# The fifth product of each quad as one 512-column product, with VectorE adding its halves, in a two-layer decoder trunk

## Chip, cores and metric

One Trainium2 chip, one core. The metric is the device time of one execution of the whole kernel in microseconds (us).

## The reference

The kernel computes a two-layer decoder trunk on 512 tokens of width 1024, batch 1, in float32. Each layer is a token mixer (layer 0: a gated linear recurrence beside dilated attention; layer 1: sliding-window attention with sinks), then cross-attention into 256 memory tokens, then a SwiGLU feed-forward block, each behind an RMSNorm and with a residual add. A last RMSNorm follows. What the change touches is the first half of the feed-forward block:

```python
def swiglu(h, w_gate_up, w_down):
    gate, up = jnp.split(h @ w_gate_up, 2, axis=-1)
    return (jax.nn.silu(gate) * up) @ w_down
```

with `h` 512 x 1024, `w_gate_up` 1024 x 5632 and `w_down` 2816 x 1024.

## The kernel before, in words

**Three products for one.** Each float32 matrix is split into a high part (rounded to the matmul's float32r) and a low part (the rest), and a product is the sum high x high + high x low + low x high. The activations are kept with tokens in the free dimension.

**Quads.** The feed-forward block of a layer works on its 22 tiles of 128 hidden columns in two chunks, of 12 and 10 tiles. The first three pairs of tiles of the first chunk are done plainly (`plain_gate`, `plain_up`, `plain_product`, `plain_low` on VectorE, `plain_silu`, `plain_high` on ScalarE). All others are done as *quads*: a quad is a product of 256 output columns (two tiles, of the gate in an even quad, of the up projection in the following odd one) by a Strassen-like scheme of seven block products instead of eight. A chunk's quads form a *run*: 6 quads in the first run of each layer, 10 in the second, 32 in all. A run is followed by the down projection of its chunk (lines 815, 818 and 819 on TensorE).

Each of the seven kinds of product multiplies sums of weight blocks (4 blocks of 128 x 128) with sums of activation blocks (4 of 128 x 256). The kinds in `APART` have the low and the high activations side by side, so that one matmul of 512 columns (line 992) gives high weights x low activations in the left half of a PSUM bank and high x high in the right half. Four matmuls of 256 columns with the low weights (line 984) follow, onto the left half. The fifth kind is not among them before: it has two matmuls of 256 columns onto the same half bank (lines 1001 and 1002), and then line 984.

**Who makes the operands.** Per quad, VectorE makes four sums of weight blocks (`weight_sum`, line 2143) and seven low parts (`weight_low`, line 2148); ScalarE makes seven high parts (`weight_high`, line 2735). VectorE then forms the two output tiles from PSUM: `first_tile` (line 2177), `second_tile` (2185) and `second_tile_apart` (2191); it multiplies gate and up (`gated`, line 2199) and takes the low part of the result (`f_low`, line 2206), twice per two quads each. ScalarE does the SiLU (line 2786), the high part of the result (line 2780) and the copies: `copy_first` (fills the left half of bank 2 with zeros, line 2744, and copies bank 1 into bank 0, line 2746), `copy_fifth` (the fifth product into `copied`, line 2762), `copy_second_sum` (the second sum's left half into `copied`, line 2767, and its right half into the right half of bank 2, line 2768), `copy_third_sum` (line 2773) and `copy_apart` (line 2754).

**The order.** It is written out by hand, one list for each engine. TensorE in a run: product 1 of quad 0, then per quad 5, 6, 2, 3, 7, product 1 of the next quad, and 4 (in the last quad 5, 6, 2, 7, 3, 4). It waits for the high and low weights of each product (`HIGH`, `LOW`), before 5 for the zeros, before 6 for the copy of the first product, before 3 (in the last quad before 7) for the second copy of the second sum, before 4 for the third sum's. VectorE's list is the loop in `quads` from line 2209: in iteration n it makes low parts 6, 3, 7 and 4 of quad n and the sums and low parts 1, 5 and 2 of quad n + 1, with the tile work between. An odd iteration has 14 instructions, an even one 18 (from the third quad on). In iteration 0 of the first run of a layer, VectorE calls `rest()`, the six instructions of the last plain pair, of which the last two, the products, wait for two SiLU; ScalarE issues these two in its own `rest()`, behind `copy_fifth`. ScalarE's list is the loop from line 2789.

The weights of a quad come in two DMAs of 512 KB (line 606), issued on SyncE when the quad before last has done with the buffer. GpSimd makes the high parts of the other weights (line 737) and does nothing within a run but its end.

Of the kernel before, what the change touches and what calls it, by code (L numbers as in the profile page):

```python
# [69 lines left out]
Z_HIGHS = (1, 2, 4, 5, 6, 7, 3)  # L70
APART = (1, 2, 3, 4, 6, 7)
Z_STEP = {slot: 2 if slot in [Z_SLOT[i] for i in APART] else 1 for slot in range(8)}
# [92 lines left out]
LOW = counts((1, 5, 2, 6, 3, 7), ((0, 6), (1, 1), (0, 3), (0, 7), (0, 4), (1, 5), (1, 2)))  # L165
COPIED = counts(("zero", "c1"), ((0, "c5"), (0, "u2"), (0, "u2d"), (0, "u3"), (1, "zero"), (1, "c1")))

# [28 lines left out]
def trunk(nc, x, mem, w_in, w_gates, w_out0, w_qkv, w_out1, xa_wq, xa_wkv, xa_wo, w_gate_up, w_down,  # L196
          vectors, gains, mask0, mask1, rope_cos, rope_sin, identity, out):
    ctx = ExitStack()
    with ctx:
# [80 lines left out]
        quad_v_lo = at("quad_v_lo", [P, 2, 4, 4, P], F32R, z_x)  # L280
        copied = at("copied", [P, 2, QHALF], F32, z_mv)
        apart = at("apart", [P, 2, QHALF], F32, z_mv + 2048)

# [524 lines left out]
        def _(pe):  # L808
# [186 lines left out]

            def quad_product(l, q, i, o):

                quad_high_ready(l, q, i)
                lo, hi = z_rows(i)
                for k in range(4):  # L1000
                    pe.matmul(o, kind_hi(i)[:, k, :], zq_r[:, hi, :][:, k, :], start=False, stop=False, skip_group_check=True)  # L1001
                    pe.matmul(o, kind_hi(i)[:, k, :], zq_r[:, lo, :][:, k, :], start=False, stop=False, skip_group_check=True)  # L1002
                quad_low_weights(q, i, o)

            def quads(l, c):

                g0, n_quads = GROUP0[f"quads{l}{c}"], QUADS[c]

                def first_product(n):

                    pe.wait_ge(s_free[(g0 + n) % 2], free_needed(g0 + n))
                    quad_product_apart(l, QUAD0[l, c] + n, 1, ps[:, bank(g0 + n, 1), :], home(g0, n, 1), True)

                first_product(0)
                for n in range(n_quads):
                    q = QUAD0[l, c] + n
                    b, a, d = home(g0, n, 0), home(g0, n, 1), home(g0, n, 2)
                    b_wide, a_wide, d_wide = (ps[:, bank(g0 + n, i), :] for i in (0, 1, 2))
                    pe.wait_ge(s_cp, COPIED[q, "zero"])
                    quad_product(l, q, 5, d)  # L1020
                    pe.wait_ge(s_cp, COPIED[q, "c1"])
                    quad_product_apart(l, q, 6, a_wide, a)
                    quad_product_apart(l, q, 2, b_wide, b)
                    if n + 1 < n_quads:
                        pe.wait_ge(s_cp, COPIED[q, "u2d"])
                        quad_product_apart(l, q, 3, d_wide, d)
                        quad_product_apart(l, q, 7, a_wide, a)
                        first_product(n + 1)
                    else:
                        pe.wait_ge(s_cp, COPIED[q, "u2d"])  # L1030
# [467 lines left out]
        def _(dve):  # L1498
# [427 lines left out]
            for l in (0, 1):  # L1926
# [236 lines left out]
                def quads(c, rest, later):  # L2163
# [4 lines left out]
                    def free(n):  # L2168

                        dve.wait_ge(s_c, 3 * (QUAD0[l, c] + n) + 3)  # L2170
                        dve.nop().then_inc(s_free[(qg + n) % 2], 4)

                    def first_tile(n):
# [3 lines left out]
                        dve.tensor_tensor(halves(ff[:, 0, :]), bank_pair(qg, n, 0), apart[:], ALU.add).then_inc(s_c, 1)  # L2177

                    def second_tile(n):

                        q = QUAD0[l, c] + n
                        ff = ff_u if n % 2 else ff_g
                        dve.wait_ge(s_p, DONE[q, 3])
                        dve.wait_ge(s_cp, COPIED[q, "u3"])
                        dve.tensor_tensor(halves(ff[:, 1, :]), bank_pair(qg, n, 2), copied[:], ALU.add).then_inc(s_c, 1)

                    def second_tile_apart(n):

                        ff = ff_u if n % 2 else ff_g
                        dve.wait_ge(s_c, 3 * (QUAD0[l, c] + n) + 1)  # L2190
                        dve.tensor_tensor(halves(ff[:, 1, :]), halves(ff[:, 1, :]), bank_pair(qg, n, 2, 1),
                                          ALU.add).then_inc(s_c, 1)

                    def gated(n, p):

                        q = QUAD0[l, c] + n
                        dve.wait_ge(s_c, 3 * q + 3 - p)
                        dve.wait_ge(s_q_silu, 2 * (q // 2) + 2 - p)
                        dve.tensor_tensor(ff_u[:, p, :], ff_g[:, p, :], ff_u[:, p, :], ALU.mult).then_inc(s_q_prod, 1)
# [9 lines left out]
                    for n in range(n_quads):  # L2209
# [33 lines left out]
                        else:  # L2243
                            low_to(down0 + 2)
                        if more:
                            weight_low(q + 1, 5)
                            if n and not up:
                                f_low(n - 1, 0)
# [76 lines left out]
        def _(act):  # L2325
# [254 lines left out]
            for l in (0, 1):  # L2580
# [156 lines left out]
                def quads(c, rest, later):  # L2737
# [3 lines left out]
                    def copy_first(n):  # L2741

                        act.wait_ge(s_free[(qg + n) % 2], free_needed(qg + n))
                        act.activation(home(qg, n, 2), cos_t[:, 0:QHALF], ACT.Copy, scale=0.0).then_inc(s_cp, 1)
                        act.wait_ge(s_p, DONE[QUAD0[l, c] + n, 1])
                        act.activation(ps[:, bank(qg + n, 0), :], ps[:, bank(qg + n, 1), :], ACT.Copy).then_inc(s_cp, 1)

                    def copy_apart(n):
# [3 lines left out]
                        if q:  # L2752
                            act.wait_ge(s_c, 3 * q)
                        act.activation(apart[:], bank_pair(qg, n, 0, 1), ACT.Copy).then_inc(s_apart, 1)

                    def copy_fifth(n):
# [3 lines left out]
                        if q:  # L2760
                            act.wait_ge(s_c, 3 * q - 2)
                        act.activation(copied[:, 1, :], home(qg, n, 2), ACT.Copy).then_inc(s_cp, 1)

                    def copy_second_sum(n):

                        act.wait_ge(s_p, DONE[QUAD0[l, c] + n, 6])
                        act.activation(copied[:, 0, :], home(qg, n, 1), ACT.Copy).then_inc(s_cp, 1)
                        act.activation(home(qg, n, 2, 1), home(qg, n, 1, 1), ACT.Copy).then_inc(s_cp, 1)

# [12 lines left out]
                    def silu(n, p):  # L2782

                        q = QUAD0[l, c] + n
                        act.wait_ge(s_c, 3 * q if p == 0 else 3 * q + 2)
                        act.activation(ff_g[:, p, :], ff_g[:, p, :], ACT.Silu).then_inc(s_q_silu, 1)

                    copy_first(0)
                    for n in range(n_quads):
# [145 lines left out]
```

## Time and profile before

| what | us |
|---|---|
| median of 3 runs | 1286.35 (1286.25 to 1286.98) |
| the profiled execution | 1286.37 |
| its span in the trace | 1284.6 |
| TensorE busy in the span | 1277.1 (99%) |
| VectorE busy | 931.2 (72%) |
| ScalarE busy | 585.5 (46%) |
| GpSimd busy | 255.6 (20%) |

Busy times count a matmul from its start to its modelled end, and instructions overlap: the time from one start to the next is shorter than the duration of one. In a timeline row the first number is the start and the second the duration, in us; a row of several instructions covers them all. L992 is line 992 of the kernel; PE is TensorE, PEld its weight load, DVE VectorE, ACT ScalarE.

### The profile page before, as it was taken

What the parts mean: (1) busy time and instruction counts of PE and PEld (TensorE: products, weight loads), DVE (VectorE), ACT (ScalarE), POOL (GpSimd) and SP (SyncE); (2) the same over time, 40 slices, a digit from 0 to 9 for tenths busy, and PEclk for the clock granted to TensorE, in tenths of its full rate; (3) what the DMA queues carried; (4) which work ended last, traced back from release to release, by engine and by line L of the source; (5) the groups of instructions that cost most, each with busy time, mean ns of one, the idle gap of its engine ahead of it and who ended that gap; (6) DMA issues with size and microseconds to landing.
All of it is one profiled execution on the core that took longest, in us unless ns stands there. A gap on an engine that the chain in (4) does not pass through costs nothing.

```text
span 1284.6 us, 18398 instructions
## 1 busy us (share of the span) xinstructions
PE 1277.1 (99%) x6780; PEld 1073.4 (84%) x6780; DVE 931.2 (72%) x1445; ACT 585.5 (46%) x1194; POOL 255.6 (20%) x290
## 2 busy tenths in 40 slices
PE   9999999999999999999999999999999999999998
PEld 7888778888888888888888878888888888888886
DVE  7887856447689994389955778557789993489942
ACT  6347356114533671067722347425433760178712
POOL 0222254312422002100021226413321002000020
PEclk9999999999999999999999999999999999999999
DMA  7334323232333333333323332132333332343222
GB/s 250 97 100 115 91 67 99 81 92 91 116 98 99 118 96 99 98 115 99 104 93 115 107 117 60 50 98 88 110 97 94 116 93 96 97 132 99 83 98 98
DMA packets 96839, 130.63 MB, mean 102 GB/s; under 512 B 5328, under 2 KB 62160, under 8 KB 96752
## 3 DMA queue, kind: packets, MB, share of 16 engines
q1 hardware_dynamic: 94976, 127.29, 31.6%
q10 hardware_dynamic: 1776, 2.18, 0.6%
q8 instruction: 54, 0.88, 0.3%
q14 instruction: 33, 0.27, 0.1%
HBM read 124.67 MB, written 2.10 MB: 99 GB/s over the span
## 4 chain that ended last, share of the span: by engine, by line
PE 98%; DVE 1%; DMA 0%; ACT 0%; SPq 0%; issue 0%; ACTq 0%; POOL 0%; DVEq 0%; POOLq 0%
PE ps L815 18%; PE ps L819 18%; PE ps L818 18%; PE ps L992 14%; PE ps L984 8%; PE ps L1480 1%; PE ps L1476 1%; PE ps L1479 1%; PE ps L1309 1%; PE ps L1002 1%; PE ps L1001 1%; PE ps L1325 1%; PE ps L1338 1%; PE ps L1198 1%; PE ps L1229 1%; PE ps L1216 1%
## 5 line engine op out<-in xcount | busy, mean ns | idle before, releaser
L737 POOL TENSOR_SCALAR w_hi<-raw 128x1024 fp32r<-128x1024 f32 x156 | 182.3, 1169 | 928.0 <-PE ps L984 360.8
L1508 DVE TENSOR_TENSOR w_lo<-raw,w_hi 128x1024 fp32r<-128x1024 f32 x161 | 198.7, 1238 | 179.9 <-POOL w_hi L737 176.7
L815 PE MATMUL ps<-f_hi,w_hi 128*128 128x512 f32 x720 | 281.1, 390 | 0.2 <-DVEq L1904 0.2
L819 PE MATMUL ps<-f_hi,w_lo 128*128 128x512 f32 x720 | 280.3, 389 | 0.0
L818 PE MATMUL ps<-f_lo,w_hi 128*128 128x512 f32 x720 | 280.2, 389 | 0.0
L992 PE MATMUL ps<-zq_r,quad_hi 128*128 128x512 f32 x768 | 209.6, 394 | 0.0
L815 PEld LDWEIGHTS ps<-f_hi,w_hi 128*128 128x128 f32 x720 | 135.2, 188 | 28.8 <-DVEq L1904 0.4
L819 PEld LDWEIGHTS ps<-f_hi,w_lo 128*128 128x128 f32 x720 | 135.1, 188 | 28.3
L818 PEld LDWEIGHTS ps<-f_lo,w_hi 128*128 128x128 f32 x720 | 135.2, 188 | 27.7
L992 PEld LDWEIGHTS ps<-zq_r,quad_hi 128*128 128x128 f32 x768 | 131.5, 189 | 17.9
L815 PE MATMUL ps<-z_hi,w_hi 128*128 128x512 f32 x304 | 120.4, 396 | 0.0
L819 PE MATMUL ps<-z_hi,w_lo 128*128 128x512 f32 x304 | 118.4, 390 | 0.0
L818 PE MATMUL ps<-z_lo,w_hi 128*128 128x512 f32 x304 | 118.3, 389 | 0.0
L2735 ACT ACTIVATE quad_hi<-quad_raw 128x512 fp32r<-128x512 f32 x96 | 60.3, 628 | 114.6 <-DMA quad_raw<-in_w_gate_up 108.4
L2148 DVE TENSOR_TENSOR quad_v_lo<-quad_v,quad_hi 128x512 fp32r<-128x512 f32 x128 | 86.1, 693 | 0.0
L984 PEld LDWEIGHTS ps<-zq_r,quad_v_lo 128*128 128x128 f32 x512 | 76.6, 190 | 8.2
L2735 ACT ACTIVATE quad_hi<-quad_v 128x512 fp32r<-128x512 f32 x128 | 76.6, 621 | 13.6 <-DVE quad_v L2143 13.5
L984 PE MATMUL ps<-zq_r,quad_v_lo 128*128 128x256 f32 x512 | 81.7, 282 | 0.0
L2336 ACT ACTIVATE z_hi<-h,vec 128x512 fp32r<-128x512 f32 x32 | 23.1, 723 | 109.9 <-DVEq L1561 108.1
L815 PEld LDWEIGHTS ps<-z_hi,w_hi 128*128 128x128 f32 x304 | 57.1, 188 | 14.8 <-issue 3.5
L819 PEld LDWEIGHTS ps<-z_hi,w_lo 128*128 128x128 f32 x304 | 57.1, 188 | 12.1
L818 PEld LDWEIGHTS ps<-z_lo,w_hi 128*128 128x128 f32 x304 | 57.1, 188 | 11.7 <-issue 0.2
(274 smaller groups left out, 2145.4 us busy)
## 6 DMA issues: line engine op xcount, KB each, us to landing
quad_raw<-in_w_gate_up SPq DMA_DIRECT2D x64, 512.0 KB
raw<-in_w_down SPq DMA_DIRECT2D x44, 512.0 KB
raw<-in_w_gate_up SPq DMA_DIRECT2D x48, 256.0 KB
raw<-in_w_out SPq DMA_DIRECT2D x20, 512.0 KB
raw<-in_w_in SPq DMA_DIRECT2D x19, 512.0 KB
raw<-in_xa_wkv SPq DMA_DIRECT2D x16, 512.0 KB
raw<-in_w_in SPq DMA_DIRECT2D x17, 256.0 KB
raw<-in_xa_wq SPq DMA_DIRECT2D x8, 512.0 KB
```

What stands on the lines that cost most here:

```text
L737: pool.tensor_scalar(w_hi[:, slot], raw[:, slot], 1.0, 1.0, ALU.mult, ALU.mult).then_inc(s_hi, 1)
L815: ins = pe.matmul(o, whi, rhi, start=start, stop=False)
L818: pe.matmul(o, whi, rlo, start=False, stop=False)
L819: return pe.matmul(o, wlo, rhi, start=False, stop=stop)
L984: ins = pe.matmul(o, kind_lo(q, i)[:, k, :], zq_r[:, hi, :][:, k, :], start=False, stop=k == 3, skip_group_check=True)
L992: pe.matmul(both, kind_hi(i)[:, k, :], low_and_high(i, k), start=start and k == 0, stop=False, skip_group_check=True)
L1001: pe.matmul(o, kind_hi(i)[:, k, :], zq_r[:, hi, :][:, k, :], start=False, stop=False, skip_group_check=True)
L1002: pe.matmul(o, kind_hi(i)[:, k, :], zq_r[:, lo, :][:, k, :], start=False, stop=False, skip_group_check=True)
L1508: dve.tensor_tensor(w_lo[:, slot], raw[:, slot], w_hi[:, slot].bitcast(F32), ALU.subtract).then_inc(s_lo, 1)
L2148: dve.tensor_tensor(kind_lo(q, i), kind_full(q, i), kind_hi(i).bitcast(F32), ALU.subtract).then_inc(s_wl, 1)
L2336: act.activation(dst[:, m, :], h[:, m, :], ACT.Identity, scale=v(f"g_{norm}", m)).then_inc(s_zh, 1)
L2735: act.activation(kind_hi(i), kind_full(q, i), ACT.Copy).then_inc(s_wh, 1)
```

## The change

Kind 5 joins `APART`: its high part becomes four matmuls of 512 columns onto both halves of bank 2, the first of them clearing it, so no zeros are written by ScalarE. `copied` has twice the size and takes both halves of the fifth product and of the second sum, by one 512-column copy each; the right half of the second sum is no longer put into bank 2. VectorE gets one instruction per quad, `copied_halves`, which adds the halves of `copied` into the second tile; `second_tile` then adds bank 2 and 3 onto that. `apart` moves to another place. On ScalarE, `rest()` moves from behind `copy_fifth` to behind `copy_second_sum`. The counts of the semaphores follow.

```diff
-APART = (1, 2, 3, 4, 6, 7)
+APART = (1, 2, 3, 4, 5, 6, 7)
...
-COPIED = counts(("zero", "c1"), ((0, "c5"), (0, "u2"), (0, "u2d"), (0, "u3"), (1, "zero"), (1, "c1")))
+COPIED = counts(("c1",), ((0, "c5"), (0, "u2"), (0, "u3"), (1, "c1")))
...
-        copied = at("copied", [P, 2, QHALF], F32, z_mv)
-        apart = at("apart", [P, 2, QHALF], F32, z_mv + 2048)
+        copied = at("copied", [P, 2, 2, QHALF], F32, z_mv)
+        apart = at("apart", [P, 2, QHALF], F32, z_const)
...
-                    pe.wait_ge(s_cp, COPIED[q, "zero"])
-                    quad_product(l, q, 5, d)
+                    quad_product_apart(l, q, 5, d_wide, d, True)
                     pe.wait_ge(s_cp, COPIED[q, "c1"])
                     quad_product_apart(l, q, 6, a_wide, a)
                     quad_product_apart(l, q, 2, b_wide, b)
                     if n + 1 < n_quads:
-                        pe.wait_ge(s_cp, COPIED[q, "u2d"])
+                        pe.wait_ge(s_cp, COPIED[q, "u2"])
                         quad_product_apart(l, q, 3, d_wide, d)
...
+                    def copied_halves(n):
+
+                        dve.wait_ge(s_cp, COPIED[QUAD0[l, c] + n, "u2"])
+                        ff = ff_u if n % 2 else ff_g
+                        dve.tensor_tensor(halves(ff[:, 1, :]), copied[:, 0, :, :], copied[:, 1, :, :], ALU.add).then_inc(s_c, 1)
...
                         dve.wait_ge(s_cp, COPIED[q, "u3"])
-                        dve.tensor_tensor(halves(ff[:, 1, :]), bank_pair(qg, n, 2), copied[:], ALU.add).then_inc(s_c, 1)
+                        dve.wait_ge(s_c, 4 * q + 1)
+                        dve.tensor_tensor(halves(ff[:, 1, :]), halves(ff[:, 1, :]), bank_pair(qg, n, 2), ALU.add).then_inc(s_c, 1)
...
                         else:
                             low_to(down0 + 2)
+                        copied_halves(n)
                         if more:
                             weight_low(q + 1, 5)
...
                     def copy_first(n):
-                        act.wait_ge(s_free[(qg + n) % 2], free_needed(qg + n))
-                        act.activation(home(qg, n, 2), cos_t[:, 0:QHALF], ACT.Copy, scale=0.0).then_inc(s_cp, 1)
...
-                        act.activation(copied[:, 1, :], home(qg, n, 2), ACT.Copy).then_inc(s_cp, 1)
+                        act.activation(copied[:, :, 1, :], halves(ps[:, bank(qg + n, 2), :]), ACT.Copy).then_inc(s_cp, 1)
...
-                        act.activation(copied[:, 0, :], home(qg, n, 1), ACT.Copy).then_inc(s_cp, 1)
-                        act.activation(home(qg, n, 2, 1), home(qg, n, 1, 1), ACT.Copy).then_inc(s_cp, 1)
+                        act.activation(copied[:, :, 0, :], halves(ps[:, bank(qg + n, 1), :]), ACT.Copy).then_inc(s_cp, 1)
...
                         copy_fifth(n)
-                        if n == 0:
-                            rest()
                         if n:
                             weight_high(c, n, 7)
                         weight_high(c, n, 4)
                         copy_second_sum(n)
+                        if n == 0:
+                            rest()
```

## Rows read from the trace of the kernel before

**Rows 1.** The page, busy time of each engine, its share of the span and instructions.

```profile
PE 1277.1 (99%) x6780; PEld 1073.4 (84%) x6780; DVE 931.2 (72%) x1445; ACT 585.5 (46%) x1194; POOL 255.6 (20%) x290
```

**Rows 2.** The page, chain that ended last, shares of the span by engine.

```profile
PE 98%; DVE 1%; DMA 0%; ACT 0%; SPq 0%; issue 0%; ACTq 0%; POOL 0%; DVEq 0%; POOLq 0%
```

**Rows 3.** Waits of TensorE: us in total, times, longest us; the longest group.

```profile
PE ps L1153 <- DVE ones_r L1722: 1.1, 1, 1.1
```

**Rows 4.** Timeline, TensorE, start of layer 0's second run, quad 0.

```profile
553.74 0.19 PEld L1001 LDWEIGHTS ps<-zq_r,quad_hi 128*128 128x128 f32 x1
553.85 0.28 PE L1001 MATMUL ps<-zq_r,quad_hi 128*128 128x256 f32 x1
...
554.81 0.64 PE L984 MATMUL ps<-zq_r,quad_v_lo 128*128 128x256 f32 x4
555.29 1.09 PE L992 MATMUL ps<-zq_r,quad_hi 128*128 128x512 f32 x4
556.22 0.63 PE L984 MATMUL ps<-zq_r,quad_v_lo 128*128 128x256 f32 x4
556.69 1.09 PE L992 MATMUL ps<-zq_r,quad_hi 128*128 128x512 f32 x4
```

**Rows 5.** Windows, two quads of layer 0's second run: busy (instructions), clock, DMA.

```profile
571.65:591.37 19.72, 19.72 (x121) 17.60 (x121) 19.33 (x32) 15.84 (x33) 0.00 (x0) 1.00 0.36 108
```

**Rows 6.** Timeline, VectorE, the same two quads and both their borders.

```profile
571.65 0.69 DVE L2185 TENSOR_TENSOR ff_u<-ps,copied 128x512 f32<-128x512 f32 x1 [1.35 <-ACT ps L2773]
...
573.46 0.69 DVE L2148 TENSOR_TENSOR quad_v_lo<-quad_v,quad_hi 128x512 fp32r<-128x512 f32 x1
...
578.87 0.69 DVE L2148 TENSOR_TENSOR quad_v_lo<-quad_v,quad_hi 128x512 fp32r<-128x512 f32 x1
...
582.48 0.68 DVE L2185 TENSOR_TENSOR ff_g<-ps,copied 128x512 f32<-128x512 f32 x1
...
591.37 0.69 DVE L2185 TENSOR_TENSOR ff_u<-ps,copied 128x512 f32<-128x512 f32 x1 [0.39 <-ACT ps L2773]
```

**Rows 7.** Timeline, ScalarE, start of layer 0's second run.

```profile
554.05 0.58 ACT L2746 ACTIVATE ps<-ps 128x512 f32<-128x512 f32 x1 [5.17 <-PE ps L984]
554.55 0.62 ACT L2735 ACTIVATE quad_hi<-quad_raw 128x512 fp32r<-128x512 f32 x1
...
556.89 0.38 ACT L2767 ACTIVATE copied<-ps 128x256 f32<-128x256 f32 x1 [0.49 <-PE ps L984]
557.17 0.38 ACT L2768 ACTIVATE ps<-ps 128x256 f32<-128x256 f32 x1
```

**Rows 8.** Timeline, VectorE, end of layer 0's first run: two dependent tile sums.

```profile
486.12 0.68 DVE L2185 TENSOR_TENSOR ff_u<-ps,copied 128x512 f32<-128x512 f32 x1
486.84 0.69 DVE L2191 TENSOR_TENSOR ff_u<-ff_u,ps 128x512 f32<-128x512 f32 x1
```

**Rows 9.** Timeline, TensorE: within runs, and the first matmuls behind them.

```profile
431.72 0.63 PE L984 MATMUL ps<-zq_r,quad_v_lo 128*128 128x256 f32 x4
...
487.15 0.40 PE L815 MATMUL ps<-f_hi,w_hi 128*128 128x512 f32 x1
...
580.15 0.64 PE L984 MATMUL ps<-zq_r,quad_v_lo 128*128 128x256 f32 x4
...
651.05 0.40 PE L815 MATMUL ps<-f_hi,w_hi 128*128 128x512 f32 x1
...
1124.07 0.28 PE L1001 MATMUL ps<-zq_r,quad_hi 128*128 128x256 f32 x1
...
1221.26 1.91 PE L1462 MATMUL ps<-ident,h 128*128 128x128 f32 x16
```

**Rows 10.** Timeline, ScalarE and VectorE, layer 0's first run, quad 0.

```profile
431.27 1.14 ACT L2705 ACTIVATE ff_g<-ff_g 128x512 f32<-128x512 f32 x2
431.93 1.29 DVE L2093 TENSOR_TENSOR ff_u<-ff_g,ff_u 128x512 f32<-128x512 f32 x2 [0.86 <-ACT ff_g L2705]
...
437.33 0.69 DVE L2185 TENSOR_TENSOR ff_g<-ps,copied 128x512 f32<-128x512 f32 x1 [0.37 <-ACT ps L2773]
```

More of the change, by code:

```diff
@@ L994, in quad_product_apart @@
                 quad_low_weights(q, i, o)
[L996 to L1003, printed above, removed]
             def quads(l, c):
@@ L1029, in quads @@
                     else:
-                        pe.wait_ge(s_cp, COPIED[q, "u2d"])
+                        pe.wait_ge(s_cp, COPIED[q, "u2"])
                         quad_product_apart(l, q, 7, a_wide, a)
@@ L2168, in free @@
                     def free(n):
-                        dve.wait_ge(s_c, 3 * (QUAD0[l, c] + n) + 3)
+                        dve.wait_ge(s_c, 4 * (QUAD0[l, c] + n) + 4)
                         dve.nop().then_inc(s_free[(qg + n) % 2], 4)
@@ L2184, in second_tile @@
                         dve.wait_ge(s_cp, COPIED[q, "u3"])
-                        dve.tensor_tensor(halves(ff[:, 1, :]), bank_pair(qg, n, 2), copied[:], ALU.add).then_inc(s_c, 1)
+                        dve.wait_ge(s_c, 4 * q + 1)
+                        dve.tensor_tensor(halves(ff[:, 1, :]), halves(ff[:, 1, :]), bank_pair(qg, n, 2), ALU.add).then_inc(s_c, 1)
                     def second_tile_apart(n):
                         ff = ff_u if n % 2 else ff_g
-                        dve.wait_ge(s_c, 3 * (QUAD0[l, c] + n) + 1)
+                        dve.wait_ge(s_c, 4 * (QUAD0[l, c] + n) + 2)
                         dve.tensor_tensor(halves(ff[:, 1, :]), halves(ff[:, 1, :]), bank_pair(qg, n, 2, 1),
@@ L2196, in gated @@
                         q = QUAD0[l, c] + n
-                        dve.wait_ge(s_c, 3 * q + 3 - p)
+                        dve.wait_ge(s_c, 4 * q + 4 - p)
                         dve.wait_ge(s_q_silu, 2 * (q // 2) + 2 - p)
@@ L2752, in copy_apart @@
                         if q:
-                            act.wait_ge(s_c, 3 * q)
+                            act.wait_ge(s_c, 4 * q)
                         act.activation(apart[:], bank_pair(qg, n, 0, 1), ACT.Copy).then_inc(s_apart, 1)
@@ L2760, in copy_fifth @@
                         if q:
-                            act.wait_ge(s_c, 3 * q - 2)
-                        act.activation(copied[:, 1, :], home(qg, n, 2), ACT.Copy).then_inc(s_cp, 1)
+                            act.wait_ge(s_c, 4 * q - 3)
+                        act.activation(copied[:, :, 1, :], halves(ps[:, bank(qg + n, 2), :]), ACT.Copy).then_inc(s_cp, 1)
                     def copy_second_sum(n):
                         act.wait_ge(s_p, DONE[QUAD0[l, c] + n, 6])
-                        act.activation(copied[:, 0, :], home(qg, n, 1), ACT.Copy).then_inc(s_cp, 1)
-                        act.activation(home(qg, n, 2, 1), home(qg, n, 1, 1), ACT.Copy).then_inc(s_cp, 1)
+                        act.activation(copied[:, :, 0, :], halves(ps[:, bank(qg + n, 1), :]), ACT.Copy).then_inc(s_cp, 1)
                     def copy_third_sum(n):
@@ L2784, in silu @@
                         q = QUAD0[l, c] + n
-                        act.wait_ge(s_c, 3 * q if p == 0 else 3 * q + 2)
+                        act.wait_ge(s_c, 4 * q if p == 0 else 4 * q + 3)
                         act.activation(ff_g[:, p, :], ff_g[:, p, :], ACT.Silu).then_inc(s_q_silu, 1)
```

## The prediction

> **What bounds the kernel now.** First the page's busy times: TensorE is busy 1277.1 of 1284.6 us [rows 1], so only a shorter stream of matmuls, or a new gap in it, can move the time. The chain of waits agrees, 98% TensorE [rows 2], and among the waits of TensorE itself [rows 3] none lies in the quad runs: the longest, 1.1 us, is at another line. All that the change touches happens in four runs of quads, 6 + 10 in each layer, 32 in all. The timeline of TensorE at the start of a run [rows 4] gives the prices. A fifth product takes 554.81 - 553.85 = 0.96 us for its eight 256-column high matmuls; a joined product takes 556.22 - 555.29 = 0.93 us for four of 512, and with its low half 556.69 - 555.29 = 1.40. A fifth product is 1.44. A quad is 1.44 + 6 x 1.40 = 9.86 us, and two are 19.72.
>
> Then the engine that is next. Over two quads of steady state [rows 5] VectorE issues 32 instructions and is busy 19.33 of 19.72 us, at a granted TensorE clock of 1.00. Its instructions follow each other every 0.601 us (573.46 to 582.48 is 15 starts, [rows 6]), though each lasts 0.69: the start-to-start time is the price, 32 x 0.601 = 19.2. The only free time in the pair is the 0.39 us before the second tile at 591.37. VectorE is therefore no hidden engine here; it is 0.4 us short of being the bound.
>
> **The change part by part.** *TensorE:* the fifth product becomes 1.40 us, so 0.04 x 32 = 1.2 us less (1.18 with unrounded starts) if TensorE goes on setting the pace; two quads then want 19.65. The rows give this price directly, since the added matmuls are the form of line 992. A sentence by itself: the Trainium skill (TensorE: Matmul & The Clock Gate, Back-to-back issue gap) gives N/2.4 + 2.5 ns, by which two halves cost 2.5 ns more than one whole and 128 pairs would give 0.3 us; the trace disagrees (0.96 against 0.93 for four) and decides.
>
> *ScalarE:* per quad it loses two copies of 256 columns, which last 0.38 and follow each other after 0.28; the two that remain grow to the 0.50 from start to start of a 512-column copy out of PSUM [rows 7]. That is 4 x 0.28 against 2 x 0.50, a little less, and ScalarE has room. The second sum's one copy ends 0.58 after the sixth product's end, where the pair ended 0.66 after it, so TensorE's wait for it gets no later of itself.
>
> *VectorE:* one more 128x512 fp32 sum per quad, both sources in SBUF. Every VectorE instruction of this size in the pair [rows 6] starts 0.60 after its forerunner, from PSUM or SBUF. I take 0.60; the other end is 0.72, the start-to-start of two instructions of which the second reads the first's result [rows 8]. The two tile sums are as many as before. So two quads hold 34 x 0.601 = 20.43 us against TensorE's 19.65: **VectorE becomes the bound and loses 0.8 us per pair.** GpSimd has none of it and stays idle in the runs.
>
> *When this reaches TensorE.* The low halves of the weights come from VectorE. The tightest is the seventh kind's in an even quad: VectorE ends it at 578.87 + 0.69 = 579.56, TensorE starts its matmul at 580.15 [rows 6, 9]. A lead of 0.59, less the response, is all there is. In a run of ten quads VectorE still waits for ScalarE before the second tile of quad 1, at 571.65, with 1.35 idle. That wait swallows the first two added sums (0.04 earlier per quad: 571.58). From there it never waits again: up to the start of the low part for the sixth product of quad 9 it has 3 instructions of quad 1, 3 x 34 for quads 2 to 7 and 19 of quad 8 (an even quad has 19 now, an odd one 15), 124 in all, 74.5 us, so 646.10. It ends 0.69 later, TensorE reacts after 0.15 (0.04 as ScalarE does, 556.22 + 0.63 to 556.89 [rows 4, 7], and 0.11 by which a weight load precedes its matmul [rows 4]; bounds 0.04 and 0.25). Then come the low half, 0.47, four products at 1.403, 5.61, and one wait of 0.21: in an odd quad ScalarE holds the fifth and second-sum copies behind the SiLU that waits for the last sum of the quad before (0.04 + 0.53 + 0.50 + 1.05 + 0.58 + 0.15 = 2.85 from its end, against 2.64 on TensorE's side). The run ends at 653.23; it ended at 651.05 [rows 9]. **2.2 us.** The second layer's run has the same length, 1124.07 to 1221.26 for 97.19, against 553.85 to 651.05.
>
> The runs of six have less room, and here the moved work counts. `rest()` holds two SiLU of the plain part, 0.52 apart; the instructions behind it on VectorE are the plain products, and behind those all weight parts. They now come after the second-sum copy, which starts when the sixth product ends: 431.72 - 0.04 + 0.67 = 432.35, SiLU at 432.85, plain product 0.66 later (431.27 to 431.93, [rows 10]) at 433.51 where it stood at 431.93. That is 1.58 late, and the 0.37 us idle at 437.33 doesn't cover it. From 433.51 to the low part of quad 5's sixth product VectorE has 14 instructions of quad 0, 15 of quad 1, 34 of 2 and 3, and 19 of quad 4, 82, of which one is dependent: 49.3 + 0.1, so 482.91. That, plus 0.69 + 0.15 + 0.47 + 5.61 + 0.21, is 490.04, against 487.15 [rows 9]. **2.9 us.** No DMA moves: the weight loads are issued on TensorE's and VectorE's counts a quad ahead, the same number. POOL's start behind a run hangs on TensorE's products and shifts with them. After each run VectorE is as far behind TensorE as before.
>
> Sum: 2 x (2.2 + 2.9) = 10.2 us on the profiled execution's own 1286.37 (its span 1284.6), which is the median, 1286.35, to 0.02: **1296.6 us**. The saving on TensorE is in it already: where VectorE paces, it is worth next to nothing. If the joined product were no faster than its halves, the sum would be 0.3 higher.
>
> **Rivals.** *The leads are enough.* TensorE keeps the pace and the time falls by 1.2 to 1285.2. This is the case on the other side, "not slower". It decides at 19.65 / 34 = 0.578 us per VectorE instruction; the rows have 0.601, and 0.39 us free where two added sums want 1.2 [rows 6]. Against it speaks every row, for it only that the leads in a short run are finite. 0.05, of which 0.02 for more than 0.2% faster.
>
> *The added sum costs its full length.* If it made its neighbours wait for results, 0.72 in place of 0.60 [rows 8], then in the stretches without waits, 7 and 5 added sums, twice, 24 x 0.12 = 2.9 more: 1299.5. Its reader stands one instruction behind it, except in the last quad of a run, which speaks against. 0.10. The Trainium skill (VectorE: DVE Perf Modes, the section on the TRN2 errata) has (N + 151)/0.96, 691 ns at 512, for an fp32 tensor sum. That agrees with the 0.69 an instruction lasts, not with the pace of 0.601; by it 24 sums would cost 2.2 more, 1298.8.
>
> *The loop closes.* ScalarE's wide copies stand behind waits for VectorE, TensorE's third product behind those copies, and VectorE's second tile behind TensorE. If VectorE then waits in turn, some 0.4 us in each of 14 pairs add 5.5: 1302.1. Against it: VectorE reaches the second tile 0.8 later per pair, while ScalarE is busy only 15.84 of 19.72 us [rows 5]. 0.08.
>
> *Half a loss.* Leads build in a way my counts miss, and only the short runs lose: 2 x 2.9, 1292.2. 0.05.
>
> **How the numbers follow.** My forecast has 0.72. The range: VectorE's pace to 0.003 over 412 instructions is 1.2 us either way, the response 0.4, the full-length rival reaches 1299.5, and the lower end goes most of the way to the half loss: 1293.5 to 1300.0, which leaves out the closed loop (0.08), the half loss and the saving (0.10). About 0.2% (2.6 us) is what a measurement of this kernel can tell from no change; by that measure slower 0.94, same 0.04, faster 0.02.
>
> **What would show it.** In the changed profile: VectorE issues 34 instructions in two steady quads and is never idle; a pair of quads takes 20.4 us where it took 19.72; TensorE has waits at line 984 for VectorE and for ScalarE's second-sum copy, some 0.4 us a quad from quad 4 of the long runs and quad 3 of the short ones on, and 1.4 in quad 1 of the short runs; the last quad run of each layer is 2.2 longer, the first 2.9. The plain product starts 1.6 later. If the pair stays at 19.65 with TensorE unbroken, the count of VectorE is wrong; if it is near 21, the loop has closed.

## The result, and the profile after

| | before | after |
|---|---|---|
| median, us | 1286.49 (1286.25 to 1286.98, 6 runs) | 1296.83 (1296.51 to 1298.17, 6 runs) |
| the profiled execution, us | 1286.37 | 1297.34 |
| its span, us | 1284.6 | 1295.6 |

The changed kernel takes 1.0082 times as long, 95% interval 1.0071 to 1.0092: 10.3 us slower by the medians. The forecast was 10.2 us and 1296.6.

The page of the changed kernel, busy times, chain by engine and two of its groups (answering to [rows 1, 2]; the groups are weight loads of TensorE, with the time it sat idle before them and what ended most of it, ScalarE's second-sum copy in the one and VectorE's low weights in the other):

```profile
PE 1284.1 (99%) x6652; PEld 1067.8 (82%) x6652; DVE 952.8 (74%) x1477; ACT 577.9 (45%) x1130; POOL 258.7 (20%) x290
...
PE 82%; DVE 12%; issue 4%; ACT 2%; DMA 0%; SPq 0%; ACTq 0%; DVEq 0%
...
L992 PEld LDWEIGHTS ps<-zq_r,quad_hi 128*128 128x128 f32 x896 | 153.2, 189 | 26.2 <-ACT copied L2763 4.7
...
L984 PEld LDWEIGHTS ps<-zq_r,quad_v_lo 128*128 128x128 f32 x512 | 77.5, 189 | 16.9 <-DVE quad_v_lo L2138 7.0
```

TensorE has 128 matmuls fewer (6652 for 6780), and VectorE 32 instructions more (1477 for 1445). In the chain VectorE rises from 1% to 12%. "PE 99%" hides this: the modelled end of a matmul bridges most small gaps, and a span with more gaps in it is still 99% busy.

Where does the time lie? The length of each run of quads, from the first matmul of product 1 to the first matmul behind the run (rows of the timelines):

| run | before | after | longer |
|---|---|---|---|
| layer 0, six quads | 59.18 | 62.08 | 2.90 |
| layer 0, ten quads | 98.58 | 100.78 | 2.20 |
| layer 1, six quads | 59.15 | 62.15 | 3.00 |
| layer 1, ten quads | 98.57 | 100.80 | 2.23 |
| sum | 315.48 | 325.81 | 10.33 |

The rest of the span is longer by 0.67 us, 0.41 of it before the first run, where the change touches nothing; the medians differ by 10.34, so that rest belongs to the one execution. Below, kernels are compared by this sum of the four runs, beside their medians.

Two quads of layer 0's second run, windows of the changed kernel, from one odd second tile to the next (answers to [rows 5]; columns: length, then busy time and instructions of PE, PEld, DVE, ACT, POOL, clock, DMA share, GB/s):

```profile
574.87:595.33 20.46, 20.46 (x118) 17.77 (x118) 20.46 (x35) 15.69 (x29) 0.00 (x0) 1.00 0.37 116
```

VectorE is busy for all of it, with 35 instructions where [rows 5] had 32; the last of them is the one at the window's end, so there are 34 from one second tile to the next. The timeline of VectorE at its borders (answers to [rows 6]):

```profile
565.04 0.69 DVE L2182 TENSOR_TENSOR ff_g<-ff_g,ps 128x512 f32<-128x512 f32 x1 [1.49 <-ACT ps L2768]
...
574.87 0.69 DVE L2182 TENSOR_TENSOR ff_u<-ff_u,ps 128x512 f32<-128x512 f32 x1 [0.72 <-ACT ps L2768]
...
594.12 0.68 DVE L2173 TENSOR_TENSOR ff_u<-copied 128x512 f32<-128x512 f32 x1
594.72 0.69 DVE L2138 TENSOR_TENSOR quad_v_lo<-quad_v,quad_hi 128x512 fp32r<-128x512 f32 x1
595.33 0.68 DVE L2182 TENSOR_TENSOR ff_u<-ff_u,ps 128x512 f32<-128x512 f32 x1
```

The last wait stands at 574.87. From there on instructions start every 0.60 us, and the pair takes (595.33 - 574.87) = 20.46 us. The added sum (L2173) costs 0.60 like its neighbours.

TensorE, timeline of the two quads behind that stretch, quad 4 of the run, an even one (first four lines), and quad 5, an odd one:

```profile
598.95 0.64 PE L984 MATMUL ps<-zq_r,quad_v_lo 128*128 128x256 f32 x4
599.43 1.09 PE L992 MATMUL ps<-zq_r,quad_hi 128*128 128x512 f32 x4
600.36 0.63 PE L984 MATMUL ps<-zq_r,quad_raw_lo 128*128 128x256 f32 x4
601.14 1.20 PE L992 MATMUL ps<-zq_r,quad_hi 128*128 128x512 f32 x4
...
608.25 1.09 PE L992 MATMUL ps<-zq_r,quad_hi 128*128 128x512 f32 x4
609.29 0.73 PE L984 MATMUL ps<-zq_r,quad_v_lo 128*128 128x256 f32 x4
609.86 1.09 PE L992 MATMUL ps<-zq_r,quad_hi 128*128 128x512 f32 x4
```

A low half takes 0.47 and a high one 0.93 undisturbed. In the even quad product 3 starts 0.78 after the low half of product 2: 0.31 of waiting, for ScalarE's second-sum copy, which ends at 601.09 (L2763, 600.50 + 0.59). ScalarE is late because a high part of the result stands ahead of its copies and waits for VectorE's product of gate and up:

```profile
598.44 0.63 ACT L2775 ACTIVATE f_hi<-ff_u 128x512 fp32r<-128x512 f32 x1 [1.02 <-DVE ff_u L2196]
```

In the odd quad the low half of product 6 starts 1.04 after its high half and lasts 0.57: 0.21 of waiting for VectorE's low weights. Such steps are read from the distances between starts: the view of waits names but two waits of TensorE for low weights in the whole kernel. One of them is in quad 1 of the first run:

```profile
440.98 1.09 PE L992 MATMUL ps<-zq_r,quad_hi 128*128 128x512 f32 x4
443.21 0.74 PE L984 MATMUL ps<-zq_r,quad_v_lo 128*128 128x256 f32 x4 [1.13 <-DVE quad_v_lo L2138]
443.78 1.09 PE L992 MATMUL ps<-zq_r,quad_hi 128*128 128x512 f32 x4
```

### The profile page after: what moved, and what is told of

Read it like the earlier page. It is cut to its first block, busy times and chain, and to the rows that moved or that the text cites. A ratio compares the mean times of both kernels' runs of the same rounds, so it can differ in the third digit from the quotient of the medians.

```text
span 1295.6 us, 18080 instructions
## 1 busy us (share of the span) xinstructions
PE 1284.1 (99%) x6652; PEld 1067.8 (82%) x6652; DVE 952.8 (74%) x1477; ACT 577.9 (45%) x1130; POOL 258.7 (20%) x290
## 4 chain that ended last, share of the span: by engine, by line
PE 82%; DVE 12%; issue 4%; ACT 2%; DMA 0%; SPq 0%; ACTq 0%; DVEq 0%
PE ps L815 18%; PE ps L819 18%; PE ps L818 18%; PE ps L992 5%; PE ps L984 3%; DVE quad_v L2133 3%; PE ps L1470 1%; PE ps L1469 1%; PE ps L1466 1%; DVE quad_v_lo L2138 1%; PE ps L1299 1%; DVE quad_raw_lo L2138 1%; PE ps L1315 1%; DVE ff_u L2196 1%; PE ps L1328 1%
## 5 line engine op out<-in xcount | busy, mean ns | idle before, releaser
L737 POOL TENSOR_SCALAR w_hi<-raw 128x1024 fp32r<-128x1024 f32 x156 | 185.4, 1190 | 934.3 <-PE ps L984 367.1
L992 PE MATMUL ps<-zq_r,quad_hi 128*128 128x512 f32 x896 | 246.6, 397 | 1.9 <-ACT copied L2763 1.1
L992 PEld LDWEIGHTS ps<-zq_r,quad_hi 128*128 128x128 f32 x896 | 153.2, 189 | 26.2 <-ACT copied L2763 4.7
```

Source lines behind the costliest of these rows:

```text
L737: pool.tensor_scalar(w_hi[:, slot], raw[:, slot], 1.0, 1.0, ALU.mult, ALU.mult).then_inc(s_hi, 1)
L992: pe.matmul(both, kind_hi(i)[:, k, :], low_and_high(i, k), start=start and k == 0, stop=False, skip_group_check=True)
```

## The experiments

The change has three parts: the joined product, the moved `rest()` and the added sum. The kernels up to the second sum take them apart; the others vary where and by whom the sum is made.

**The added sum left out.**

```diff
-                        dve.wait_ge(s_c, 4 * q + 1)
-                        dve.tensor_tensor(halves(ff[:, 1, :]), halves(ff[:, 1, :]), bank_pair(qg, n, 2), ALU.add).then_inc(s_c, 1)
+                        dve.tensor_tensor(halves(ff[:, 1, :]), bank_pair(qg, n, 2), copied[:, 0, :, :], ALU.add).then_inc(s_c, 1)
...
-                        copied_halves(n)
```

> The changed kernel without the sum of the two halves on VectorE: the second tile takes the left half of what was copied and leaves out the right half (the high x high parts of the fifth product and of the second sum). The joined product, both wide copies and the moved SiLU stay. Theory (VectorE's instruction count sets the pace): with 32 instructions in two quads TensorE paces again. Against the kernel before, a run of ten quads is 0.3 us shorter, a run of six 0.5 us longer (the moved SiLU), the whole +0.5: 1287.0 us; two quads of steady state take 19.65 us. Rival (the wide copies on ScalarE or the joined product cost the time): it stays within 2 us of 1296.8.

Measured: 1286.97 us (10 runs), ratio 1.0003 (0.9993 to 1.0013); runs 59.68, 98.21, 59.78, 98.21, sum 315.88. All but 0.4 of the 10.3 us (by the sum of the four runs) are gone with the one instruction per quad. Windows of this kernel, two quads of the same run:

```profile
572.48:592.13 19.65, 19.65 (x113) 17.17 (x113) 19.33 (x32) 15.46 (x29) 0.00 (x0) 1.00 0.36 108
```

Two quads take the 19.65 us that the joined product allows TensorE, and VectorE has 0.3 free again.

**`rest()` put back behind `copy_fifth`,** the rest of the change kept.

```diff
                         copy_fifth(n)
+                        if n == 0:
+                            rest()
...
-                        if n == 0:
-                            rest()
```

> The changed kernel with the two SiLU of the last plain pair put back behind the copy of the fifth product, all else as changed. Theory (the 1.5 us by which the plain product is late cannot be made good, since VectorE has no free time): runs of six get 1.4 us shorter each, runs of ten stay as they are: 1296.8 - 2.8 = 1294.0 us. Rival (the move is hidden, the added sum alone costs): 1296.8 us, nothing changes.

Measured: 1293.96 (4 runs), ratio 1.0059 (1.0042 to 1.0076); runs 60.70, 100.77, 60.78, 100.76, sum 323.01. The short runs get back 1.4 each, the long ones nothing.

**The kernel before with one sum added** per quad, into a tile that nobody reads.

```diff
+                            dve.wait_ge(s_cp, COPIED[q, "u2"])
+                            dve.tensor_tensor(halves(acc[:]), copied[:], copied[:], ALU.add)
```

> The kernel before with one more 128x512 sum on VectorE per quad, at the place of the change's, its result unused. Nothing else of the change. Theory: runs of ten are 2.1 us longer than before, runs of six 1.2, the whole 6.5: 1293.0 us, and two quads of steady state take 34 x 0.601 = 20.4 us. Rival (it takes the joined product or the wide copies to lose the time): 1286.5 us. Rival (each added sum costs 0.72 where it stands): 1295.5 us or more.

Measured: 1293.34 (4 runs), ratio 1.0052 (1.0036 to 1.0069); runs 60.36, 100.71, 60.44, 100.69, sum 322.20. An instruction whose result nobody needs costs 6.7 us: it is VectorE's time, and not a wait for the sum.

**The kernel before with `rest()` moved** as the change moves it.

> The kernel before with only the two SiLU moved behind the second sum's copies. Theory: runs of six 0.8 us longer each, runs of ten as they are, the whole 1.6: 1288.1 us. Rival (hidden while VectorE has free time): 1286.5 us.

Measured: 1288.02 (11 runs), ratio 1.0013 (1.0004 to 1.0022); runs 59.97, 98.57, 60.03, 98.58, sum 317.15, 1.67 more, all in the short runs.

**The joined product alone:** no sum, and `rest()` put back.

> The joined product alone: no added sum on VectorE, and rest() where it was before. It leaves out the right halves of the fifth product and of the second sum. If the three parts of the change add up (product, moved work, added sum), this one is the sum-free kernel less the price of the moved work: 1286.97 - 1.67 = 1285.3 us, that is 1.2 below before (32 products at 0.04), with run lengths 58.9, 98.2, 58.9, 98.2. Rival: the joined product saves nothing by itself, because TensorE has other small waits that take its place; then it is at 1286.5 like the kernel before, with run lengths 59.2, 98.6.

Measured: 1285.73 (11 runs), ratio 0.9995 (0.9986 to 1.0004); runs 59.09, 98.20, 59.09, 98.20, sum 314.58. The long runs have the 0.37 that was expected, the short ones only 0.07 of 0.24. The timeline of TensorE in quad 0 of this kernel's first run shows why:

```profile
432.89 0.63 PE L984 MATMUL ps<-zq_r,quad_raw_lo 128*128 128x256 f32 x4
433.45 1.19 PE L992 MATMUL ps<-zq_r,quad_hi 128*128 128x512 f32 x4
434.48 0.64 PE L984 MATMUL ps<-zq_r,quad_raw_lo 128*128 128x256 f32 x4
```

and of ScalarE:

```profile
432.81 0.59 ACT L2755 ACTIVATE copied<-ps 128x512 f32<-128x512 f32 x1
```

With `rest()` ahead of it, the second-sum copy ends at 433.40, and product 3, due at 433.36, starts at 433.45 and takes 0.10 more. That is the wait which moving `rest()` removes, 0.2 us per short run; the move itself costs 0.8. By the median this kernel is no faster than before beyond what can be told.

**A second sum beside the first,** unused, in the changed kernel.

```diff
                         copied_halves(n)
+                        dve.tensor_tensor(halves(acc[:]), copied[:, 0, :, :], copied[:, 1, :, :], ALU.add)
```

> The changed kernel with the sum of the halves issued a second time on VectorE, into an unused place: the suspected cost doubled. Theory (the first added sum was partly absorbed by VectorE's free time before the first tiles of a run, a second one finds none left): runs of ten 6.4 us longer than before the change, runs of six 5.9, the whole 24.6: 1311.1 us; two quads take 36 x 0.601 = 21.6 us. Rival (cost proportional to the number of sums): 1296.8 + 10.3 = 1307.1 us. Rival (VectorE is not the pace): 1296.8 us.

Measured: 1312.56 (4 runs), ratio 1.0202 (1.0186 to 1.0218); runs 65.31, 105.19, 65.38, 105.20, sum 341.08, 15.3 more than the change. That is 1.5 us over the expected 1311.1; all four runs have a share in it, and its cause was not tried. Windows, two quads:

```profile
577.90:599.56 21.66, 21.35 (x121) 18.21 (x121) 21.66 (x37) 16.21 (x31) 0.00 (x0) 1.00 0.36 113
```

36 starts at 0.602. The second sum costs 15.3 where the first cost 9.9 (325.81 - 315.88): the free time of VectorE is spent only once, which rules out a cost in proportion to the number of sums.

**The sum directly ahead of its reader,** in place of one (odd quads) or two (even quads) instructions between them.

```diff
-                        copied_halves(n)
                         if more:
                             weight_low(q + 1, 5)
...
+                        copied_halves(n)
```

> The changed kernel with the sum of the halves moved two or three instructions later on VectorE, to stand directly before the second tile's sum, which reads its result. Same instructions, same count. Theory (a reader right behind starts after 0.72 us instead of 0.60): runs of ten 3.0 us longer than before the change, runs of six 3.5, the whole 13.0: 1299.5 us. Rival (only the count matters): 1296.8 us.

Measured: 1304.66 (4 runs), ratio 1.0143 (1.0126 to 1.016); runs 63.79, 102.92, 64.22, 102.91, sum 333.84, 8.0 more than the change. Both expectations were too low. Timelines of this kernel, first VectorE, then GpSimd:

```profile
586.90 0.69 DVE L2173 TENSOR_TENSOR ff_g<-copied 128x512 f32<-128x512 f32 x1
587.72 0.69 DVE L2182 TENSOR_TENSOR ff_g<-ff_g,ps 128x512 f32<-128x512 f32 x1
...
651.61 0.68 DVE L2188 TENSOR_TENSOR ff_g<-ff_g,ps 128x512 f32<-128x512 f32 x1
652.21 1.45 DVE L2138 TENSOR_TENSOR quad_v_lo<-quad_v,quad_hi 128x512 fp32r<-128x512 f32 x1
653.58 0.68 DVE L2138 TENSOR_TENSOR quad_raw_lo<-quad_raw,quad_hi 128x512 fp32r<-128x512 f32 x1
```

```profile
652.07 1.05 POOL L737 TENSOR_SCALAR w_hi<-raw 128x1024 fp32r<-128x1024 f32 x1 [111.83 <-PE ps L984]
```

The reader starts 0.82 after the sum, 0.22 more than the pace, where [rows 8] have 0.72. And in front of the last quad VectorE's low part at 652.21 holds its successor for 1.37 in place of 0.60, while GpSimd makes the first high weights of the down projection beside it; the same stretch stands in the other three runs, at 483.98, 1063.67 and 1231.90. TensorE waits for that low part. In a long run the sums of quads 2 to 8 stand behind no wait: 7 x 0.22 + 0.77 - 0.21 (TensorE's wait for the copy is covered now) = 2.1, against 2.14 and 2.11 measured; in a short one 5 x 0.22 + 0.77 - 0.21 = 1.7, against 1.71 and 2.07. Of the 8.0 us some 0.4, in layer 1's short run, isn't in this account. It stands in one place, quad 3 of that run, where the reader starts 1.16 after the sum and not 0.82; what held it is not shown:

```profile
1049.05 0.68 DVE L2173 TENSOR_TENSOR ff_u<-copied 128x512 f32<-128x512 f32 x1
...
1050.21 0.69 DVE L2182 TENSOR_TENSOR ff_u<-ff_u,ps 128x512 f32<-128x512 f32 x1 [0.49 <-DVE ff_u L2173]
```

In the changed kernel the same two instructions miss each other. Timelines of it, VectorE and then GpSimd:

```profile
649.45 0.69 DVE L2138 TENSOR_TENSOR quad_v_lo<-quad_v,quad_hi 128x512 fp32r<-128x512 f32 x1
...
651.25 1.54 DVE L2138 TENSOR_TENSOR quad_v_lo<-quad_v,quad_hi 128x512 fp32r<-128x512 f32 x2
```

```profile
649.54 2.11 POOL L737 TENSOR_SCALAR w_hi<-raw 128x1024 fp32r<-128x1024 f32 x1 [110.47 <-PE ps L984]
```

GpSimd's instruction starts 0.09 after the low part for the sixth product, which keeps its 0.60 to the next, and lasts 2.11 in place of 1.05. It stretches two later low parts, 1.54 for the 1.29 that two take elsewhere, for which TensorE doesn't wait.

**The same, with GpSimd later:** its first high part behind a run waits for the last quad's sixth product in place of the fifth.

```diff
-                    pool.wait_ge(s_p, DONE[quads - 1, (5, 2, 3, 4)[j]])
+                    pool.wait_ge(s_p, DONE[quads - 1, (6, 2, 3, 4)[j]])
```

> The kernel with the sum directly ahead of its reader, and one edit: GpSimd's first high part of the down projection waits for the last quad's sixth product in place of its fifth. If GpSimd stretches VectorE's low part for that sixth product (the next start comes 1.37 later, not 0.60), this stretch leaves the place where TensorE waits for it, each of the four runs gets 0.77 us back, and the sum of the four goes from 333.84 to 330.8; the median from 1304.66 to 1301.6. Rival: the long low part has another cause (its own wait for ScalarE's high part); then it stays at 1.45 us and the median at 1304.7, or rises, since GpSimd's high parts come later. Second rival: it is gone, but TensorE then waits for the down projection's high weights by as much; then VectorE's row is short and the time is still 1304 to 1305.

Measured: 1302.68 (4 runs), ratio 1.0124 (1.0107 to 1.0141); runs 63.22, 102.36, 63.65, 102.35, sum 331.58. Timelines of VectorE and GpSimd:

```profile
652.26 0.68 DVE L2138 TENSOR_TENSOR quad_v_lo<-quad_v,quad_hi 128x512 fp32r<-128x512 f32 x1
652.86 0.69 DVE L2138 TENSOR_TENSOR quad_raw_lo<-quad_raw,quad_hi 128x512 fp32r<-128x512 f32 x1
653.47 0.68 DVE L2167 TENSOR_TENSOR ff_g<-ps,apart 128x512 f32<-128x512 f32 x1
654.07 2.94 DVE L2138 TENSOR_TENSOR quad_v_lo<-quad_v,quad_hi 128x512 fp32r<-128x512 f32 x2
```

```profile
653.96 1.06 POOL L737 TENSOR_SCALAR w_hi<-raw 128x1024 fp32r<-128x1024 f32 x1 [113.66 <-PE ps L984]
```

The low part at 652.26 is back at 0.60, and the stretch has moved with GpSimd to the rows at 654.07, for which TensorE doesn't wait. Each run gets 0.56 or 0.57 back and not 0.77: the wait of 0.21 for the copy, which the long low part had covered, is there again. The expectation had left it out.

**One 1024-column instruction** adds both halves of banks 2 and 3 into `copied`, and a second adds the halves; `rest()` is put back. The count of VectorE is that of before.

```diff
+                        both = ps[:, bank(qg + n, 2):bank(qg + n, 2) + 2, :].rearrange("p h (s n) -> p s h n", s=2)
+                        dve.tensor_tensor(copied[:], both, copied[:], ALU.add).then_inc(s_c, 1)
```

> The joined product with the second tile made otherwise: one VectorE instruction of 1024 columns adds both halves of banks 2 and 3 onto what ScalarE copied, one of 512 adds the halves; so two instructions of 1.13 and 0.60 us in place of three of 0.60. The two SiLU are back behind the copy of the fifth product. Theory (VectorE's time in the stretches without waits counts, 0.07 us less per quad; but all of it now stands behind the wait for TensorE, where the added sum was partly absorbed before): runs of ten 2.2 us longer than before the change, runs of six 1.5, the whole 7.4: 1293.9 us, as with the two SiLU back alone. Rival (the number of instructions counts, not their time): 32 in two quads as before the change, 1286 us.

Measured: 1294.05 (4 runs), ratio 1.006 (1.0043 to 1.0077); runs 60.74, 100.88, 60.75, 100.87, sum 323.24, that of the kernel with `rest()` put back (323.01) to 0.2. What counts is the columns, not the instructions: the wide one lasts 1.22 and its successor starts 1.14 later.

**The sum by GpSimd,** which does nothing in the runs; `rest()` put back.

```diff
+                        pool.wait_ge(s_cp, COPIED[QUAD0[l, c] + n, "u2"])
+                        pool.tensor_tensor(copied[:, 0, :, :], copied[:, 0, :, :], copied[:, 1, :, :], ALU.add).then_inc(s_halves, 1)
```

> The joined product as changed, but the sum of the two halves made by GpSimd in place (in a run it has nothing else to do but at the end), and the two SiLU back behind the copy of the fifth product. VectorE has 32 instructions in two quads as before. Theory: TensorE paces, the 1.2 us of the joined product come out but for the edges of the runs: 1285.8 us, 0.7 below the kernel before. Rival (GpSimd's sum slows VectorE's instructions beside it, or is late for the second tile): 1288 us or more, with VectorE's start-to-start time over 0.601 us while GpSimd works.

Measured: 1308.01 (4 runs), ratio 1.0168 (1.0151 to 1.0185); runs 63.08, 105.09, 63.18, 105.13, sum 336.48. It is slower than even the change: the theory is out, and the rival holds, 20 us beyond its least price. The group in the page of this kernel, and its timelines of GpSimd and VectorE:

```profile
L809 POOL TENSOR_TENSOR copied<-copied 128x512 f32<-128x512 f32 x32 | 108.4, 3388 | 273.3 <-ACT copied L2763 273.3
```

```profile
603.04 6.22 POOL L809 TENSOR_TENSOR copied<-copied 128x512 f32<-128x512 f32 x1 [9.31 <-ACT copied L2763]
614.04 1.29 POOL L809 TENSOR_TENSOR copied<-copied 128x512 f32<-128x512 f32 x1 [4.78 <-ACT copied L2763]
```

```profile
607.43 0.68 DVE L2204 TENSOR_TENSOR f_lo<-ff_u,f_hi 128x512 fp32r<-128x512 f32 x1
609.39 0.69 DVE L2183 TENSOR_TENSOR ff_g<-ps,copied 128x512 f32<-128x512 f32 x1 [1.28 <-POOL copied L809]
...
614.21 1.68 DVE L2140 TENSOR_TENSOR quad_v<-quad_raw,quad_v 128x512 f32<-128x512 f32 x1
615.81 0.68 DVE L2145 TENSOR_TENSOR quad_v_lo<-quad_v,quad_hi 128x512 fp32r<-128x512 f32 x1
```

A sum of 1.29 us on GpSimd is held for 6.22 while VectorE issues without a pause, and ends only when VectorE itself stops to wait for it (idle 1.28). Where it comes through at once, VectorE's next instruction is followed after 1.60 in place of 0.60. Against the sum on VectorE (1293.96) the 32 sums on GpSimd cost 14.1 us more.

**An unused GpSimd instruction beside the kernel before,** with two sources, and with one.

```diff
+                        pool.tensor_tensor(halves(acc[:]), halves(cos_t[:]), halves(sin_t[:]), ALU.add).then_inc(s_halves, 1)
```

> The kernel before with one 128x512 sum of two SBUF tensors on GpSimd in each quad but the last of a run, beside VectorE, for whose result nobody waits: what the sum on GpSimd costs by its presence alone. Theory (GpSimd and VectorE exclude each other on two-source instructions: a GpSimd sum stretches the VectorE instruction that it meets by 1.0 us, as one row of the run before showed, 1.68 for 0.68): VectorE loses about 1 us in each quad where it has 0.2 free, about 1300 to 1305 us. Rival (it was only the wait for GpSimd's late result): 1286.5 us.

> As the run before, but GpSimd's instruction is a scaling of one SBUF tensor of the same size. Theory (only two-source instructions exclude each other): 1286.5 us, no VectorE instruction over 0.70 us beside it. Rival (any GpSimd instruction disturbs): as the run with two sources.

Measured, two sources: 1292.56 (4 runs), ratio 1.0046 (1.003 to 1.0061), sum 321.59. That is 6.1 us for the company of 28 instructions, well under the expected 1300 to 1305, so the price was put too high; that it costs nothing is excluded. One source: 1286.8 (10 runs), ratio 1.0002 (0.9993 to 1.0011), sum 315.47, as its theory has it. Timelines of the first, GpSimd and VectorE:

```profile
579.00 6.64 POOL L810 TENSOR_TENSOR acc<-cos_t,sin_t 128x512 f32<-128x512 f32 x1 [5.63 <-ACT copied L2775]
589.11 1.30 POOL L810 TENSOR_TENSOR acc<-cos_t,sin_t 128x512 f32<-128x512 f32 x1 [3.48 <-ACT copied L2775]
```

```profile
584.40 0.68 DVE L2193 TENSOR_TENSOR ff_g<-ps,copied 128x512 f32<-128x512 f32 x1
585.00 1.18 DVE L2156 TENSOR_TENSOR quad_raw_lo<-quad_raw,quad_hi 128x512 fp32r<-128x512 f32 x1
586.11 0.68 DVE L2199 TENSOR_TENSOR ff_g<-ff_g,ps 128x512 f32<-128x512 f32 x1
```

The instruction asked for at 579.00 ends at 585.64, 1.24 after VectorE has started one that reads PSUM (584.40); the one at 589.11 starts with a VectorE instruction that reads PSUM too, and takes 1.30. VectorE's next instruction, with two sources in SBUF, pays for it: here 0.5 to 0.6 (585.00 to 586.11 is 1.11 where the pace is 0.60), and 1.0 in the kernel with the sum on GpSimd. No data and no signal passes between the two here: the mere company costs it.

## Why the prediction was right

**The bound.** The forecast was that 34 instructions at 0.601 (20.43 us) take TensorE's place (19.65) as the pace of two quads. Measured 20.46, with the 34 and no pause of VectorE. Doubling the sum gives 21.66, which is 36 instructions at 0.602. Leaving it out gives 32, which would be 19.2, and the pair takes TensorE's 19.65.

**The long runs.** Forecast +2.2: from the fifth product of quad 0 to the end of the run 653.23 - 553.85 = 99.38; measured 656.56 - 557.16 = 99.40. The second tile of quad 1 was put at 571.58 - 553.85 = 17.73 behind the run's fifth product and stands at 17.71, with 0.72 free in front of it. The two added sums there cost nothing, as forecast.

**The short runs.** Forecast +2.9; measured 2.90 and 3.00. The plain product starts at 433.91; less the 0.41 by which the run starts later (428.38 for 427.97) that is the forecast 433.51 to 0.01:

```profile
433.91 1.29 DVE L2083 TENSOR_TENSOR ff_u<-ff_g,ff_u 128x512 f32<-128x512 f32 x2 [2.23 <-ACT ff_g L2703]
```

**The parts.** In sums of the four runs: joined product -0.9, the sum on top of it +8.4, the moved work on top of both +2.8. The order matters: without the sum the move costs 1.3, since VectorE still has free time that takes up a part. The forecast counted the move inside the short runs' 2.9, which was the right way to do it. Its words on the joined product's saving, "where VectorE paces, it is worth next to nothing", hold: with one sum per quad and `rest()` in its old place, the kernel with the joined product stands at 323.01 and the one with the old product at 322.20. The joined one is even 0.8 longer, most of it in the short runs; why was not tried.

**The waits of TensorE.** Forecast some 0.4 a quad. In quad 5, an odd one, they are where the working has them: 0.21 at the sixth product's low weights, and as much again at its product 3 (start 611.37, next 612.40), behind the second-sum copy. In quad 4, an even one, all 0.42 stands before product 3 and in its first matmuls (0.78 - 0.47, and 0.11). There ScalarE's copies stand behind a high part of the result, while the prediction has them late in odd quads only, behind a SiLU. The low weights that it calls the tightest, the seventh kind's in an even quad, show no wait in quad 4. Its lengths don't hang on this, since each run ends in an odd quad. In quad 1 of the short run there is 1.3 + 0.1, forecast as 1.4.

**Slips that change nothing.** From the printed terms, 1.44 + 6 x 1.40 is 9.84 and not 9.86, and 0.04 x 32 is 1.28 and not 1.2; both results are those of unrounded starts (1.403 and 0.037), and the 19.72 and 19.65 of a pair are measured. The 0.58 and 0.66 "after the sixth product's end" count from the start of the copy, 0.04 later.

**The rivals.** That leads are enough is excluded by every run with the sum; the loop of waits didn't close (20.46, not 21). Half a loss is out too, since each long run lost 2.2 us. That the sum costs its full length fell in the changed kernel, where the reader stands one instruction later, but the kernel with the sum directly ahead of its reader shows that its premise was sound, and its price even low: 0.22, not 0.12.

The Trainium skill (VectorE: DVE Perf Modes, "The DRAIN you can't avoid") says that the next Vector instruction doesn't start until the pipeline of the one before is empty, and that one which is not held starts earlier. The traces agree with the second half: 0.60 from start to start for durations of 0.68. The added sum at 594.12 is such a case: its successor starts at 594.72.

What the prediction had not seen at all is GpSimd's part at the run's end. It did no harm in the changed kernel, and that is luck: in each of the four runs it starts only 0.07 to 0.09 after the low part that TensorE waits for. A little earlier it would in all likelihood have met that one, as it does with the sum ahead of its reader (0.77 a run).

## What to carry to other kernels

Where a second engine is within a few per cent of the bound, count its instructions by their start-to-start time over one period of the loop, and compare with the same period of the first engine: 34 x 0.601 against 19.65 gave the result to 0.1 us, while the busy shares over the whole span (99% and 72%) show nothing of it. Moving work from the bounding engine to such a neighbour is paid from the neighbour's free time first, and in full behind that. A step that lets the neighbour start later, as the moved `rest()` does, is paid from the same free time, so the two add up to more than their prices alone (2.8 in place of 1.3). An idle third engine is no free place for the work, unless a run shows that the two don't hold each other up.

## What the runs showed of the hardware

GpSimd and VectorE hold each other up. (The profile calls its GpSimd spans rough; the starts of VectorE's rows move at the same moments.) A GpSimd instruction of 0.62 us (one source) or 1.30 us (two sources), asked for while VectorE issues instructions with two SBUF sources one behind another, was held for up to 6.6 us in all, until VectorE issued one with a source in PSUM or stopped; one behind such an instruction came through at once. The one-source GpSimd instruction was held as well, 5.97 us in the first row below. VectorE's next instruction paid nothing behind that one (583.49 to 584.09), and 0.1 behind the one at 587.34, which came through at once (587.69 to 588.42):

```profile
577.48 5.97 POOL L810 TENSOR_SCALAR acc<-cos_t 128x512 f32<-128x512 f32 x1 [6.30 <-ACT copied L2775]
587.34 0.62 POOL L810 TENSOR_SCALAR acc<-cos_t 128x512 f32<-128x512 f32 x1 [3.89 <-ACT copied L2775]
```

```profile
587.69 0.80 DVE L2151 TENSOR_TENSOR quad_v<-quad_raw,quad_v 128x512 f32<-128x512 f32 x1
588.42 0.68 DVE L2156 TENSOR_TENSOR quad_v_lo<-quad_v,quad_hi 128x512 fp32r<-128x512 f32 x1
```

The Trainium skill (SBUF — State Buffer, "SBUF: two separate sides") describes an exclusive lock on a pair of ports that GpSimd shares with VectorE instructions of two SBUF inputs, held by whichever starts first for its whole instruction. The traces agree that one keeps the other out, GpSimd for up to 5.3 us beyond its own time. They show besides that back-to-back instructions of VectorE leave GpSimd no turn between them.

A VectorE instruction right behind the one whose result it reads started 0.72 after it in [rows 8] and 0.82 in the kernel with the sum ahead of its reader, where it waits for two more signals as well. The changed kernel's last quads have 0.81 for the same pair. Whether the added signals make the 0.10 was not tried.
